# One reciprocal and one product of the HGRN2 mixer, issued one lane sooner

## The reference

```python
q = jax.nn.silu(zq)                      # z * 1 / (1 + exp(-z))
f = lbh + (1.0 - lbh) * jax.nn.sigmoid(zf)
k = 1.0 - f                              # log_f = log(f)
...
b = jnp.cumsum(ln, axis=2)               # inside a chunk
q_dec = qn * jnp.exp(b)
k_inv = kn * jnp.exp(-b)
a = jnp.where(causal, jnp.einsum('bhtk,bhsk->bhts', q_dec, k_inv), 0.0)
o = a @ vn + q_dec @ S
S_new = exp(b_last) * S + (kn * jnp.exp(b_last - b))^T @ vn
```

## Time and profile before

| | before |
|---|---|
| median of 3 runs | 2329.79 us (2329.49 to 2330.51) |
| time of the profiled execution | 2330.02 us |
| its span, first to last instruction | 2328.3 us |
| mean granted PE clock | 0.999 |
| PE busy | 2315.5 us (99%) |
| DVE, ACT, POOL busy | 1190.6, 776.2, 295.2 us |

### The profile page before, as it was taken

The page is one execution under the profiler, slowest core; times in us unless marked ns, Lnnn a source line. Parts: engine busy times, 40 slices in busy tenths (PEclk is TensorE's granted clock), DMA queues, the critical chain, the costliest instruction groups (busy, mean ns, idle before and its releaser), DMA issues.

```text
span 2328.3 us, 29589 instructions
## 1 busy us (share of the span) xinstructions
PE 2315.5 (99%) x10976; PEld 1941.3 (83%) x10976; DVE 1190.6 (51%) x1392; ACT 776.2 (33%) x1050; POOL 295.2 (13%) x269
## 2 busy tenths in 40 slices
PE   9999999999999999999999999999999999999998
PEld 9988888888888888888888888888888888888887
DVE  6554443367888554444345444337438644444422
ACT  5532222244555332222233223224433223222322
POOL 3400001201334320000220000220001122000000
PEclk9999999999999999999999999999999999999999
DMA  7733333332222333333333333332232233333322
GB/s 237 226 94 95 99 97 111 99 91 64 80 74 82 101 98 99 91 98 99 96 94 99 93 96 118 98 95 80 81 100 82 89 93 109 97 92 99 99 91 91
DMA packets 400724, 234.34 MB, mean 101 GB/s; under 512 B 7724, under 2 KB 386704, under 8 KB 400656
## 3 DMA queue, kind: packets, MB, share of 16 engines
q1 hardware_dynamic: 397328, 223.37, 32.4%
q0 software_dynamic: 3312, 10.02, 1.2%
q10 hardware_dynamic: 16, 0.00, 0.0%
HBM read 227.07 MB, written 6.29 MB: 100 GB/s over the span
## 4 chain that ended last, share of the span: by engine, by line
PE 97%; DVE 1%; ACT 1%; POOL 0%; DMA 0%; issue 0%; SPq 0%; ACTq 0%; POOLq 0%; DVEq 0%
PE acc L1126 27%; PE acc L1128 27%; PE acc L1127 27%; PE acc L879 1%; PE acc L880 1%; PE acc L881 1%; PE acc L263 1%; PE acc L265 1%; PE acc L264 1%; PE mix L265 1%; PE mix L263 1%; PE mix L264 1%; PE acc L1171 1%; PE acc L1172 1%; PE acc L1170 1%; PE mix L946 1%
## 5 line engine op out<-in xcount | busy, mean ns | idle before, releaser
L1293 DVE TENSOR_TENSOR w_lo<-raw,w_hi 128x1024 fp32r<-128x1024 f32 (+1 forms) x422 | 526.0, 1249 | 645.9 <-ACT w_hi L1562 634.3
L1126 PE MATMUL acc<-h_hi,w_hi 128*128 128x512 f32 x1920 | 751.8, 392 | 0.0
L1128 PE MATMUL acc<-h_hi,w_lo 128*128 128x512 f32 x1920 | 747.7, 389 | 0.0
L1127 PE MATMUL acc<-h_lo,w_hi 128*128 128x512 f32 x1920 | 747.7, 389 | 0.0
L1562 ACT ACTIVATE w_hi<-raw 128x1024 fp32r<-128x1024 f32 (+1 forms) x422 | 437.3, 1039 | 458.9 <-DMA raw<-in_ffn_w_out_dram 269.6
L1128 PEld LDWEIGHTS acc<-h_hi,w_lo 128*128 128x128 f32 x1920 | 360.6, 188 | 75.7
L1127 PEld LDWEIGHTS acc<-h_lo,w_hi 128*128 128x128 f32 x1920 | 360.9, 188 | 73.8 <-issue 0.2
L1126 PEld LDWEIGHTS acc<-h_hi,w_hi 128*128 128x128 f32 x1920 | 360.9, 188 | 73.4 <-issue 0.2
L1126 PE MATMUL acc<-act_hi,w_hi 128*128 128x512 f32 (+1 forms) x976 | 367.4, 376 | 1.3 <-DVE w_lo L1293 0.8
L1128 PE MATMUL acc<-act_hi,w_lo 128*128 128x512 f32 (+1 forms) x976 | 365.6, 375 | 0.0
L1127 PE MATMUL acc<-act_lo,w_hi 128*128 128x512 f32 (+1 forms) x976 | 365.6, 375 | 0.0
(11 more groups left out here) (253 smaller groups left out, 1890.3 us busy)
## 6 DMA issues: line engine op xcount, KB each, us to landing
raw<-in_ffn_w_in_dram SPq DMA_DIRECT2D x176, 512.0 KB, 3.7
raw<-in_ffn_w_out_dram SPq DMA_DIRECT2D x70, 512.0 KB, 3.5
raw<-in_hgrn_w_in_dram SPq DMA_DIRECT2D x40, 512.0 KB, 3.7
raw<-in_gmlp_w_in_dram SPq DMA_DIRECT2D x40, 512.0 KB, 3.6
raw<-in_mem_w_kv_dram SPq DMA_DIRECT2D x32, 512.0 KB, 4.6
raw<-in_gmlp_w_out_dram SPq DMA_DIRECT2D x24, 512.0 KB, 3.4
raw<-in_ffn_w_out_dram SPq DMA_DIRECT2D x24, 384.0 KB, 3.0
raw<-in_hgrn_w_out_dram SPq DMA_DIRECT2D x16, 512.0 KB, 3.4
```

Source lines behind the costliest of these rows:

```text
L1126: pe.matmul(bank, top[:, i, :], hi, start=(start and i == 0), stop=False)
L1127: pe.matmul(bank, top[:, i, :], lo, start=False, stop=False)
L1128: m = pe.matmul(bank, rest[:, i, :], hi, start=False, stop=(stop and i == last))
L1293: dve.tensor_tensor(lane_of(w_lo, q, j)[:, 0:nkb], lane_of(raw, q, j)[:, 0:nkb], f32(lane_of(w_hi, q, j)[:, 0:nkb]), ALU.subtract).then_in ...
```

## The change

The reciprocal of the query's denominator goes from the end of DVE's lane 3 to the end of its lane 2, behind the forget gate's affine step. The product that makes q goes with it, from POOL's lane 3 to the end of its lane 2. The product that makes qdec stays in lane 3 and moves up from fifth to second place, behind kinv. No wait is dropped and no shape is changed.

```diff
@@ vector, j == 2, own: behind the affine step of the forget gate
+                        dve.wait_ge(sem("q_den"), h + 1)
+                        dve.reciprocal(tmp[:, 1, :], tmp[:, 1, :]).then_inc(sem("q_sig"), 1)
@@ vector, j == 3, own: at the end
-                    dve.wait_ge(sem("q_den"), h + 1)
-                    dve.reciprocal(tmp[:, 1, :], tmp[:, 1, :]).then_inc(sem("q_sig"), 1)
@@ pool, j == 2, own: behind k = 1 - f
+                    pool.wait_ge(sem("q_sig"), h + 1)
+                    pool.tensor_tensor(self.q, tmp[:, 0, :], tmp[:, 1, :], ALU.mult).then_inc(sem("q_ready"), 1)
@@ pool, j == 3, own
                     pool.tensor_tensor(self.kinv, self.k, self.enb, ALU.mult).then_inc(sem("qdec_ready"), 1)
+                    pool.wait_ge(sem("q_ready"), h + 1)
+                    pool.tensor_tensor(self.qdec, self.q, self.eb, ALU.mult).then_inc(sem("qdec_ready"), 1)
                     pool.wait_ge(sem("rest_exp"), h + 1)
                     ... cross part, odd half of khat ...
-                    pool.wait_ge(sem("q_sig"), h + 1)
-                    pool.tensor_tensor(self.q, tmp[:, 0, :], tmp[:, 1, :], ALU.mult).then_inc(sem("q_ready"), 1)
-                    pool.wait_ge(sem("q_ready"), h + 1)
-                    pool.tensor_tensor(self.qdec, self.q, self.eb, ALU.mult).then_inc(sem("qdec_ready"), 1)
                     pool.wait_ge(sem("k_cross_ready"), h + 1)
```

## The result

The changed kernel takes 2348.39 us (median of 6, 2347.33 to 2348.65) against 2329.64 us for the kernel before (6 executions), a ratio of 1.0078 with a 95% interval of 1.0067 to 1.0089. It is slower by 18.8 us; 2346 was forecast, in a range of 2336 to 2352.

A forecast was written before the change was run, and what follows sets the result against it. DVE's round trip of 30.05 us a head was to replace PE's 27.17 as the bound, making head 8 16.3 us later; added to the profiled 2330.0, itself 0.2 over the median, this gave 2346 us, range 2336 to 2352.

The forecast's parts named there:

- What bounds: Mixer heads: PE leads before at 27.17 us a head; after, DVE's round trip of 30.05 us bounds seven heads.
- The chain behind the scan: Lane 3, scan's end through kinv, qdec, `lo` and khat products to L644: 6.4 us, bounds 5.34 and 6.4.
- The hold on the squares: Lane 2: POOL's q product holds DVE's L689, so L692 starts 2.78 us after `lo`, some 0.95 late.
- Who goes next: POOL and DVE instructions reading SBUF block each other; whoever waits goes next, before the other's second: 2346 us by turns.
- Sum: Head 0 to head 8: PE's khat transpose in head 8's quad starts 16.3 us later, giving 2346 us.
- before unit 2: One of several places in each head where PE was to idle; no size of its own was given.
- Signs that I named: Profile after: L644 waits 1.5 us or more a head, heads 30.05 us apart, PE waits 2.9 us a head.
- One block only: Rival: only the hold on L689 or the one in lane 3 costs; 2338 to 2339 us, 22%.
- none: Rival: neither hold between POOL and DVE costs; DVE's round trip 28.0 us, total +1.2, 2331 us, 10%.
- PE staying the bound: Rival: L644 finds khat ready, DVE's trip under 27.17 us, only head 1's stop goes: -3.6, 2326 us, 4%.
- did the clock fall: Rival: each head's PE stops halve the clock, PE losing 1.6 us more a head; 2348 to 2357 us, 12%.
- the ring through PE: Not in the prediction: scan's end, POOL's late qdec, PE's attention product, DVE's L669, next scan's end; 28.4 us.

The follow-up runs named there:

- Experiment 5: Changed kernel with half of the moved reciprocal left out (256 of 512 columns), for its time only: 2336.46 us, ratio 1.0027 to the kernel before.
- 3: Changed kernel with L644 writing the gate to its own tile, so it no longer waits there for khat: 2337.17 us, ratio 1.0028 to the kernel before.
- experiment 2: Changed kernel with qdec put back to fifth place in POOL's lane 3, reciprocal and q product still moved: 2340.14 us, ratio 1.0042 to the kernel before.
- experiment 9: Changed kernel with the gate's own tile, and qdec also waiting until lane 3's `lo` is done: 2332.6 us, ratio 1.0008 to the kernel before.
- Experiment 1: Only the reciprocal moved to lane 2, POOL in the order of the kernel before: 2340.94 against 2330.27 us, ratio 1.0045.
- experiment 4: Changed kernel with POOL's q product also waiting until DVE's low part of the squares is done: 2345.7 us, ratio 1.0066 to the kernel before.
- experiment 7: Kernel before plus a second, unused reciprocal in DVE's lane 2, the needed one left in place: 2342.04 us, ratio 1.0053 to the kernel before.
- experiment 6: New order for head 0 only, heads 1 to 7 in the order of the kernel before: 2330.15 against 2330.08 us, ratio 1.0000.
- 8: New order for head 0 only, plus the gate's own tile for L644: 2329.39 against 2330.78 us for the kernel before, ratio 0.9996.

## Why the prediction was right, step by step

**What bounds.** Right, and shown: with PE's idle time at 2.1 us a head and its clock full, the pace was DVE's. Experiment 5 cuts DVE alone and the heads follow; 3 takes one wait of DVE away and they follow.

**The chain behind the scan.** L644 was forecast at 6.4 us behind the scan's end and stands at 627.40 - 620.99 = 6.41. Of the parts, experiment 2 prices the moved qdec (1.25 us) and 3 the wait (1.5 a head); 9 takes the hold away, 1.1 in `lo` itself and 0.75 a head.

**The hold on the squares.** Forecast 2.78 us from `lo` to L692 (now L694); measured 619.18 - 616.43 = 2.75. Experiments 1 and 4 show the product to be the cause, and 4 that moving it a little wins only 0.4 us a head.

**Who goes next.** The rule of turns, read off rows 10 and 11, held at every place shown above: product, DVE, product. It is read off the rows; only experiment 9 turned one of the turns round.

**Sum.** 16.3 us to head 8's L609, and 16.3 measured; that they agree to the tenth is partly luck, since 0.16 us of it had come before the mixer began (L466 starts at 483.45 and 485.06). The medians lie 2.5 us further apart than the sum. In the profiles, that is the 0.9 behind that point, of which the stop for `lo` (0.68) was named in the prediction (PE's idle "before unit 2") but not in the sum, and the start of the program, 1.45 us, where the prediction has no term. If that start were chance alone, one would expect the medians 16.3 + 0.9 = 17.2 us apart; they are 18.8, in an interval of 15.6 to 20.7, which doesn't decide it.

**Signs that I named.** L644's wait was to be 1.5 us or more and is 1.4; PE's stops 2.9 us a head and are 1.4 + 0.3 + 0.4 = 2.1 of idle time, though the heads are 30.01 - 27.17 = 2.8 us longer. The difference is the overlap of matmuls that a stop takes away (0.68 us for 0.43 of idle time above) and the slower first matmul behind it (L632 0.50 instead of 0.39). Neither changes the argument.

**The rivals.** One block only, or none, falls with the two held instructions, both seen. PE staying the bound falls with the 30.0 us. Nor did the clock fall: in all windows of the mixer the granted clock is 1.00, the higher level, though PE stopped three times in each round. The windows of three rounds (the granted clock is the third number from the end):

```profile
618.00:648.00 30.00, 27.86 (x142) 22.84 (x142) 25.77 (x23) 13.87 (x21) 12.10 (x12) 1.00 0.24 70
648.00:678.00 30.00, 27.87 (x142) 22.84 (x142) 25.78 (x23) 13.87 (x21) 12.10 (x12) 1.00 0.24 70
678.00:708.00 30.00, 27.91 (x142) 22.84 (x142) 25.79 (x23) 13.87 (x21) 12.12 (x12) 1.00 0.24 70
```

The Trainium skill says, on page "TensorE: Matmul & The Clock Gate", section "What's actually happening", that the chip sets this clock by how busy PE has been. The rows above agree with it: PE was busy for 27.9 of 30 us, and the clock stayed at the higher level.

**What the prediction lacked**, without harm to it, is the ring through PE. Experiment 1 missed by it (10.7 us for the 1 to 3 expected), 7 was forecast with it and came out on it. That DVE's lateness at head 1, 1.6 us from the reciprocal's new place and more from L644's wait, would come back as a stop at head 2 was missed as well (experiments 6 and 8).

Open: where the last 0.2 us behind head 8 come from, and whether the start of the program differs between kernels by more than chance; neither was tried.

## What to carry to other kernels

When an instruction is moved earlier on an engine, ask what it lay under before: here a reciprocal of 3.3 us filled exactly the time in which DVE would have waited for ACT and POOL, and in its new place it found only 1.6 us of idle time, while the old place stayed empty. Add up each ring that a loop closes, start to start, also those that go out through another engine and come back, and compare them with the engine that leads; a busy share of 51% says nothing of it. And a stop of an engine that leads can be cured only if the others aren't made later by the cure, or it comes back one round on.

## What the runs showed of the hardware that I had not expected

- The block between POOL and DVE takes in the scan: it took 1.93 us beside a product of POOL and 1.21 without (experiment 4). Instructions with one operand in PSUM (L644 and L694, 0.68 us) and the reciprocal (3.35 us) were not held by any.
- A lead of 0.07 us decides a turn: `lo`, issued 0.07 us behind qdec, lost 1.1 us, and then POOL's next product lost 1.0 to it. An added wait that gave the first turn to `lo` (experiment 9) took both away.
- The clock: stops of 1.97 us (experiment 2), 1.98 (the kernel before), 3.3 (experiment 1) and 3.4 us (experiment 7), all at head 1, were each followed by windows of 2 us with a granted clock of 0.50 to 0.55, the lower of the two levels; a stop of 1.74 us at head 2 (experiment 6), and the shorter ones in the mixer of all runs, were followed by 1.00.
